# Moving the slices of a dense projection one step later among the attention steps that they fill

## Chip, cores and metric

The kernel runs on one core of one Trainium2 chip. The metric is the device time of one execution in microseconds (us), as the median of several runs.

## What is computed

One inference step of a two-layer encoder trunk, for two groups of requests (512 prompt frames and 32 sample frames) that share one set of weights. In each layer the mixer sub-layer makes one wide input projection and feeds it to three branches; cross-attention and a dense feed-forward follow. The part that matters here is the first branch, attention with a forget gate, over 8 heads of 64, and the input projection beside it:

```python
a_q, a_k, a_v, a_f, b_q, b_k, b_v, c_in, gate_in = _split_cols(h @ w_in, IN_SPLITS)
...
log_f = jax.nn.log_sigmoid((a_f + fox_forget_bias).astype(f32))
d_all = jnp.cumsum(jnp.concatenate([fox_lf0.astype(f32), log_f], axis=1), axis=1)
...
s = jnp.einsum('bqhd,bkhd->bhqk', qb, k_all).astype(jnp.float32) * scale
s = s + jnp.swapaxes(dqb, 1, 2)[:, :, :, None] - d_k[:, :, None, :]
mask = kpos[None, None, None, :] <= pb[:, None, :, None]
p = jax.nn.softmax(jnp.where(mask, s, -jnp.inf), axis=-1)
return jnp.einsum('bhqk,bkhd->bqhd', p.astype(v_all.dtype), v_all)
```

Only the columns `a_q, a_k, a_v, a_f` of the input projection are needed by this branch. The columns of the other two branches are computed later, and the kernel calls them the late projection.

## The kernel before

The program is written by hand for each engine: each engine has its own list of instructions, in order, and the lists meet only at semaphores. Nothing reorders the work, so the place of a call in the Python loops is its place in its engine's queue.

**The attention stage.** Heads go in pairs, four pairs (`it` = 0 to 3) in each of two layers. A pair has ten score tiles, `FOX_TILES`: for each of its two heads four blocks of 128 prompt queries (against 128, 256, 384, 512 keys) and one of 32 sample queries (against 544 keys). TensorE (PE) goes through 13 steps, k = 0 to 12:

- `fox_prologue(k)` in steps 0 and 1: three groups of transposes ("jobs": L882, L887, L891) that bring a head's values, keys and cached keys into place. ScalarE (ACT) copies each group out of PSUM. Jobs alternate between banks 4 and 5, so each waits for the copy of the job two before it (`fx_put`).
- `fox_scores(k)` in steps 0 to 9 (L904, L905, L910 to L912). The first tile of a head waits for `fx_scaled`, the scaling of that head's queries by VectorE (DVE), L2136.
- `late(s)`: a slice of the late projection, below.
- `fox_turn(k - 2)` in steps 2 to 11: transposes of the normalised probabilities (L922, L926).
- `fox_values(...)` in steps 4, 7, 8, 10 and 12 (L940, L945, L948): the products with the values. Each waits for ACT's copies of the turned probabilities.

Between PE's steps DVE takes each tile's maximum (`fox_max`, L2122), ACT the exponentials (`fox_exp`, L1423), and DVE the division by the sum (`fox_norm`, L2129, L2131). After a pair, DVE copies its output to `brT` (`fox_evac`, L2141, L2142).

**The late projection.** It has 26 units of 128 output columns. Of each, every half of the frames is one accumulation in bank 7 of PSUM, in two slices of 12 matmuls (L858). ACT copies a finished half out (`late_put(q)`, L1426), and the next half may not begin before that (`late_evac`). Each unit's weights are split by DVE into a high and a low part (`late_split`, L1932 and L1942) into one of two buffers, so a unit's split waits for the last slice of the unit two before it (`late_done`). Twelve slices go with each pair. Slice 0 of pair 0 is ahead of the loop.

**In the first pair only**, DVE also clears rows of the second set of buffers at step 3, behind the split that stands there (L2158, L2159).

**DVE's order at a pair's end** is: the last split of the pair (`late_split(3 * it + 2)`), `fox_evac`, then `fox_scale(0)` of the next pair, which `fox_scores(0)` of that pair waits for.

Of the kernel before, what the change touches and what calls it, by code (L numbers as in the profile page):

```python
# [162 lines left out]
def build_program(nc, A, C_const, C_rope, O):  # L163
# [7 lines left out]
    with ExitStack() as ctx:  # L171
# [257 lines left out]
        def half(t, h):  # L429
            return t[:, h * HT:(h + 1) * HT]  # L430
# [221 lines left out]
        def _(pe):  # L652
# [142 lines left out]
            for l in range(DEPTH):  # L795
# [6 lines left out]
                def of_h_split(k):  # L802
                    return HH[:, k, :], hTR[:, k, :]
# [42 lines left out]
                def late(s):  # L846

                    n, h, k0 = s // 4, s % 4 // 2, s % 2 * 4
                    v = V_LATE + n
                    if k0 == 0:  # L850
                        if h == 0:
                            pe.wait_ge(split_done, l * SPLITS + v + 2)
                        pe.wait_ge(late_evac, l * 2 * N_LATE + 2 * n + h + 1)
                    for k in range(k0, k0 + 4):
                        xhi, xlo = of_h_split(k)
                        whi, wlo = (w[:, v % 2, k, :] for w in (WHI, WLO))
                        for i, (w, x) in enumerate(((whi, xhi), (whi, xlo), (wlo, xhi))):
                            ins = mm(PS[:, 7, 0:HT], w, half(x, h), start=(k == 0 and i == 0), stop=(k == 7 and i == 2))  # L858
                    if k0 == 4:
                        ins.then_inc(late_done, 1)  # L860
# [5 lines left out]
                for it in range(FOX_HEADS // 2):  # L866
# [49 lines left out]
                    def fox_turn(k):  # L916
                        h, i = FOX_TILES[k]
                        pe.wait_ge(fx_norm, g * 10 + k + 1)
                        b = put_bank()
                        if i < 4:  # L920
                            for t in range(i + 1):
                                ins = tr(b[:, t * P:(t + 1) * P], FP[:, k % 3, t * P:(t + 1) * P], ident)  # L922
                        else:
                            for t in range(5):
                                w = P if t < 4 else DEC_SEQ
                                ins = tr(b[0:w, t * 32:(t + 1) * 32], FP[0:32, k % 3, t * P:t * P + w],  # L926
                                         ident[0:32, 0:32])
                        ins.then_inc(fx_turned, 1)
# [24 lines left out]
                    for k in range(13):  # L953
                        if k < 2:
                            fox_prologue(k)
                        if k < 10:
                            fox_scores(k)
                        if k < (12 if it else 11):
                            late(12 * it + k + (0 if it else 1))
                        if 2 <= k <= 11:  # L960
                            fox_turn(k - 2)
                        if k in FOX_VALUES:
                            fox_values(FOX_VALUES[k])
# [457 lines left out]
        def _(act):  # L1421
# [3 lines left out]
            def copy(out, in_):  # L1425
                return act.copy(out, in_)  # L1426
# [62 lines left out]
            for l in range(DEPTH):  # L1489
# [45 lines left out]
                def late_put(q):  # L1535

                    act.wait_ge(late_free, l * 2 * N_LATE + q + 1)
                    act.wait_ge(late_done, l * 2 * N_LATE + q + 1)
                    copy(ESTL[:, q % 4, :], PS[:, 7, 0:HT]).then_inc(late_evac, 1)

                for it in range(FOX_HEADS // 2):
                    g = l * 4 + it
                    job = [0]

                    def next_job():
                        j = job[0]
                        job[0] += 1
                        act.wait_ge(fx_turned, g * 16 + j + 1)
                        return PS[:, 4 + j % 2, :]

                    def fox_prologue(h):
                        for to in (FVT, FKT):
                            b = next_job()
                            copy(to[it % 2][:, h, 0:4, :].rearrange("p a b -> p (a b)"), b[:, 0:256])
                            copy(to[it % 2][0:DEC_SEQ, h, 4, :], b[0:DEC_SEQ, 256:320])
                            act.drain().then_inc(fx_put, 1)
                        b = next_job()
                        copy(FK[it % 2][0:64, h, T:T + PAST], b[0:64, :]).then_inc(fx_put, 1)

                    def fox_exp(k):  # L1560
                        i = FOX_TILES[k][1]
                        act.wait_ge(fx_max, g * 10 + k + 1)
                        m, n = (P, (i + 1) * P) if i < 4 else (DEC_SEQ, T)
                        f(FP[0:m, k % 3, 0:n], bank_on(k % 3)[0:m, 0:n], ACT.Exp, bias=FST[0:m, k % 3, 0:1],
                          accum_out=FST[0:m, k % 3, 1:2])
                        act.drain().then_inc(fx_exp, 1)

                    def fox_put(k):
                        i = FOX_TILES[k][1]
                        b = next_job()  # L1570
                        if i < 4:
                            copy(FPT[:, FOX_SLOT[k], 0:(i + 1) * P], b[:, 0:(i + 1) * P]).then_inc(fx_put, 1)
                        else:
                            copy(FPT[:, FOX_SLOT[k], 0:P], b[:, 0:P])
                            copy(FPT[0:32, FOX_SLOT[k], P:P + 32], b[0:32, P:P + 32])
                            act.drain().then_inc(fx_put, 1)

                    for k in range(12):
                        if k < 2:
                            fox_prologue(k)  # L1580
                        if k < 10:
                            fox_exp(k)
                        if k % 2 == (1 if it else 0):
                            late_put(6 * it + k // 2)
                        if k >= 2:
                            fox_put(k - 2)

# [284 lines left out]
        def _(dve):  # L1873
# [148 lines left out]
            for l in range(DEPTH):  # L2022
# [92 lines left out]
                for it in range(FOX_HEADS // 2):  # L2115
                    g = l * 4 + it

                    def fox_max(k):
                        h, i = FOX_TILES[k]
                        m, n = (P, (i + 1) * P) if i < 4 else (DEC_SEQ, T)  # L2120
                        dve.wait_ge(fx_scores, g * 10 + k + 1)
                        dve.tensor_reduce(FST[0:m, k % 3, 0:1], bank_on(k % 3)[0:m, 0:n], AX.X, ALU.max,  # L2122
                                          negate=True).then_inc(fx_max, 1)

                    def fox_norm(k):
                        h, i = FOX_TILES[k]
                        m, n = (P, (i + 1) * P) if i < 4 else (DEC_SEQ, T)
                        dve.wait_ge(fx_exp, g * 10 + k + 1)
                        dve.reciprocal(FST[0:m, k % 3, 2:3], FST[0:m, k % 3, 1:2])  # L2129
                        dve.drain()  # L2130
                        ts(FP[0:m, k % 3, 0:n], FP[0:m, k % 3, 0:n], FST[0:m, k % 3, 2:3], None, ALU.mult) \  # L2131
                            .then_inc(fx_norm, 1)

                    def fox_scale(h):
                        dve.wait_ge(fx_loaded[it % 2][h], (l * 2 + it // 2 + 1) * 16 * 7)
                        ts(FQ[it % 2][0:64, h, :], FQ[it % 2][0:64, h, :], HEAD_DIM ** -0.5, None, ALU.mult).then_inc(fx_scaled, 1)  # L2136

                    def fox_evac():

                        dve.wait_ge(fx_out, g + 1)  # L2140
                        copy(brT[:, it, 0:SEQ], PS[:, 6, :])  # L2141
                        copy(brT[:, it, SEQ:T], PS[:, 3, 64:96])  # L2142
                        dve.drain().then_inc(fx_evac, 2)

                    for k in range(11):
                        if k < 2:
                            fox_scale(k)
                        if k < 10:
                            fox_max(k)
                        if k >= 1:  # L2150
                            fox_norm(k - 1)
                        if k in (3, 9):
                            late_split(3 * it + k // 9)
                        if (it, k) == (0, 3):

                            dve.wait_ge(est_free, l * 12 + 16)
                            dve.wait_ge(lf_stored, (l + 1) * 64)
                            dve.memset(FQ[1][64:66, :, :], 1.0)  # L2158
                            dve.memset(FK[1][64:66, :, :], 1.0)  # L2159
                            dve.drain().then_inc(fx_rows, 1)  # L2160
                    late_split(3 * it + 2)
                    fox_evac()
# [703 lines left out]
```

## Time and profile before

| | |
|---|---|
| median of 3 runs | 2830.41 us (2828.62 to 2831.1) |
| the profiled execution's own time | 2827.76 us |
| its span, first to last instruction | 2826.0 us |
| mean granted TensorE clock | 0.992 |
| PE busy | 2703.9 us, 96% of the span |
| DVE busy | 1686.9 us, 60% |
| ACT busy | 756.6 us, 27% |
| POOL (GpSimd) busy | 244.8 us, 9% |

A row of the profile names an engine, a line of the kernel, the operation, what it writes and reads, and how many instructions were merged into it. In brackets stands how long the engine sat idle before it, and who released it.
### The profile page before, as it was taken

The page shows a single profiled execution, that of the slowest core. Times are in us where ns is not written, and L with a number is a line of the kernel's source. Part 1 is how long each engine was busy: PE and PEld are TensorE (multiplying, and loading weights), DVE is VectorE, ACT ScalarE, POOL GpSimd, SP SyncE. Part 2 cuts the span into 40 slices and gives each one's busy share as a digit, 9 for nine tenths or more (in the row PEclk, how much of TensorE's full clock was granted, in tenths as well). Part 3 has the DMA queues.
Part 4 walks back from the last instruction along what each step waited for, and adds up shares of the span by engine and source line. Part 5 has one row for each costly group of instructions (what it writes and reads, how often), then busy time and mean ns, then how long its engine had stood idle before and what let it go on. Part 6 is the DMA issues. An engine that isn't in the chain of part 4 may idle for free.

```text
span 2826.0 us, 63638 instructions
## 1 busy us (share of the span) xinstructions
PE 2703.9 (96%) x26656; PEld 2539.9 (90%) x26656; DVE 1686.9 (60%) x3101; ACT 756.6 (27%) x1813; POOL 244.8 (9%) x423
## 2 busy tenths in 40 slices
PE   8999999999999989999999999999999998999998
PEld 7877889999999789999988788899999996999998
DVE  6544565666666476664484455556666656666634
ACT  2143343333232330000123433433233324200001
POOL 1221112000000100000002221110000000000000
PEclk9999999999999999999999999999999999999999
DMA  5543436222263222333335444442224532233331
GB/s 159 143 126 105 141 107 168 73 73 66 83 172 112 56 82 86 87 88 89 83 98 139 111 136 138 84 157 73 73 69 117 155 98 75 71 87 90 87 89 59
DMA packets 421293, 290.29 MB, mean 103 GB/s; under 512 B 38560, under 2 KB 387392, under 8 KB 420880
## 3 DMA queue, kind: packets, MB, share of 16 engines
q1 hardware_dynamic: 399024, 228.64, 29.3%
q0 software_dynamic: 21984, 57.59, 6.5%
q8 instruction: 211, 3.46, 0.5%
q14 instruction: 74, 0.61, 0.1%
HBM read 232.12 MB, written 54.07 MB: 101 GB/s over the span
## 4 chain that ended last, share of the span: by engine, by line
PE 76%; DVE 11%; DVEq 4%; ACT 3%; DMA 3%; issue 2%; ACTq 0%; SPq 0%
PE PS L762 35%; PE PS L858 10%; PE PS L1161 8%; PE PS L1094 7%; DMA U<-gate_scratch 2%; ACT U L1423 2%; PE PS L904 1%; PE PS L1135 1%; PE PS L1303 1%; PE PS L783 1%; ACT U L1426 1%; DVE WLO L1942 1%; PE PS L940 1%; DVE U_r L1932 1%; PE PS L1019 1%
## 5 line engine op out<-in xcount | busy, mean ns | idle before, releaser
L762 PE MATMUL PS<-U_r,WHI 128*128 128x272 f32 x3008 | 538.5, 290 | 17.0 <-DVEq L2449 9.5
L1932 DVE CAST WHI<-ring 128x1024 fp32r<-128x1024 f32 (+2 forms) x262 | 175.3, 669 | 485.2 <-PE PS L762 372.2
L762 PEld LDWEIGHTS PS<-U_r,WHI 128*128 128x128 f32 x3008 | 438.5, 189 | 23.8 <-DVEq L2449 13.8
L1426 ACT COPY U<-PS 128x272 f32<-128x272 f32 (+8 forms) x770 | 267.5, 372 | 661.8 <-PE PS L1161 140.0
L762 PE MATMUL PS<-brT_r,WHI 128*128 128x272 f32 x1920 | 398.1, 289 | 7.5 <-DVEq L1944 6.1
L762 PE MATMUL PS<-U_r,WLO 128*128 128x272 f32 x1728 | 357.1, 288 | 0.0
L762 PE MATMUL PS<-hT_r,WHI 128*128 128x272 f32 x1600 | 330.6, 288 | 0.0
L1942 DVE TENSOR_TENSOR WLO<-ring,WHI 128x1024 fp32r<-128x1024 f32 (+2 forms) x262 | 308.3, 1177 | 20.6 <-issue 0.9
L762 PE MATMUL PS<-brT_r,WLO 128*128 128x272 f32 x1536 | 318.3, 289 | 0.0
L762 PEld LDWEIGHTS PS<-brT_r,WHI 128*128 128x128 f32 x1920 | 301.5, 188 | 10.1 <-DVEq L1944 7.6
L858 PE MATMUL PS<-U_r,WHI 128*128 128x272 f32 x832 | 260.7, 313 | 12.3 <-ACT U L1426 12.1
L762 PEld LDWEIGHTS PS<-U_r,WLO 128*128 128x128 f32 x1728 | 271.5, 189 | 0.0
L762 PEld LDWEIGHTS PS<-hT_r,WHI 128*128 128x128 f32 x1600 | 251.6, 189 | 0.0
L858 PE MATMUL PS<-U_r,WLO 128*128 128x272 f32 x832 | 241.1, 290 | 0.0
L858 PE MATMUL PS<-hT_r,WHI 128*128 128x272 f32 x832 | 240.2, 289 | 0.0
L762 PEld LDWEIGHTS PS<-brT_r,WLO 128*128 128x128 f32 x1536 | 239.9, 189 | 0.0
L1094 PE MATMUL PS<-U_r,WHI 128*128 128x272 f32 x768 | 230.1, 300 | 2.8 <-DVEq L2244 2.4
L1094 PE MATMUL PS<-U_r,WLO 128*128 128x272 f32 x768 | 221.6, 289 | 0.0
L1094 PE MATMUL PS<-hT_r,WHI 128*128 128x272 f32 x768 | 220.9, 288 | 0.0
L1161 PE MATMUL PS<-U 64*64 64x64 f32 (+1 forms) x5184 | 213.2, 239 | 0.0
L1161 PEld LDWEIGHTS PS<-U 64*64 64x64 f32 x5184 | 207.2, 134 | 1.2 <-issue 0.6
L858 PEld LDWEIGHTS PS<-U_r,WHI 128*128 128x128 f32 x832 | 158.5, 190 | 31.4 <-issue 15.0
(351 smaller groups left out, 4106.0 us busy)
## 6 DMA issues: line engine op xcount, KB each, us to landing
ring<-in_w_in_dram SPq DMA_DIRECT2D x126, 512.0 KB, 4.4
ring<-in_w_ffn_in_dram SPq DMA_DIRECT2D x88, 512.0 KB, 3.8
ring<-in_w_ffn_out_dram SPq DMA_DIRECT2D x32, 448.0 KB, 3.5
proj_scratch<-U POOLq DMA_DIRECT2D x104, 136.0 KB, 2.1
U<-proj_scratch SPq DMA_DIRECT2D x48, 272.0 KB, 4.7
ring<-in_w_branch_dram SPq DMA_DIRECT2D x48, 256.0 KB, 3.3
gate_scratch<-U POOLq DMA_DIRECT2D x88, 136.0 KB, 3.2
U<-gate_scratch SPq DMA_DIRECT2D x44, 272.0 KB, 2.9
```

Of the source, the lines that this page charges most:

```text
L762: ins = mm(PS[:, 2 * q + h, 0:HT], w, half(x, h), start=(first and k == 0 and n == 0), stop=(last and k == kn - 1 and n == len(terms) - 1))
L783: ins = mm(PS[:, 2 * j + h, 0:HT], w, half(x, h), start=(k == 0 and n == 0), stop=(k == KM - 1 and n == 2))
L858: ins = mm(PS[:, 7, 0:HT], w, half(x, h), start=(k == 0 and i == 0), stop=(k == 7 and i == 2))
L904: mm(PS[:, b, 0:n], q, FK[it % 2][0:66, h, 0:n], start=True, stop=False)
L940: ins = mm(PS[o, 6, i * P:(i + 1) * P], FVT[it % 2][:, h, t, :], pt[:, t * P:(t + 1) * P], start=(t == 0), stop=(t == i))
L1019: mm(PS[:, b, 0:n], DQ[h][r, i * P:(i + 1) * P], DK[h][r, 0:n], start=True, stop=False)
L1094: ins = mm(PS[:, 6 + h, 0:HT], w, half(x, h), start=(k == 0 and i == 0), stop=(k == 7 and i == 2))
L1161: ins = mm(PS[r, bank, cols], w_c[r], x_c[r], start=(n == 0), stop=(n == len(pairs) - 1))
L1423: return act.activation(out, in_, func, **kw)
L1426: return act.copy(out, in_)
L1932: copy(hi, src)
L1942: tt(lo, w, hi.bitcast(F32), ALU.subtract)
```

## The change

The slices of a pair are moved among PE's steps. In pairs 1 to 3 they stood in steps 0 to 11 and now stand in steps 1 to 12. In pair 0 they stood in steps 0 to 10 and now stand in steps 2 to 12. Their number and order are the same. A slice now stands in front of the values of step 12. ACT's copies of the finished halves follow: they were in the odd steps (even ones in pair 0) and are now in steps 2, 4, ... 12 of each pair. The pair's first split on DVE goes from step 3 to step 5; the other two keep their places.

```diff
@@ PE @@
-                        if k < (12 if it else 11):
-                            late(12 * it + k + (0 if it else 1))
+                        if k >= (1 if it else 2):
+                            late(12 * it + k - 1)
                         if 2 <= k <= 11:
                             fox_turn(k - 2)
                         if k in FOX_VALUES:
@@ ACT @@
-                    for k in range(12):
+                    for k in range(13):
                         if k < 2:
                             fox_prologue(k)
                         if k < 10:
                             fox_exp(k)
-                        if k % 2 == (1 if it else 0):
-                            late_put(6 * it + k // 2)
-                        if k >= 2:
+                        if k >= 2 and k % 2 == 0:
+                            late_put(6 * it + k // 2 - 1)
+                        if 2 <= k < 12:
                             fox_put(k - 2)
@@ DVE @@
-                        if k in (3, 9):
+                        if k in (5, 9):
                             late_split(3 * it + k // 9)
```

## Rows read from the trace of the kernel before

**Rows 1.** The page: the chain that ended last, by engine.

```profile
PE 76%; DVE 11%; DVEq 4%; ACT 3%; DMA 3%; issue 2%; ACTq 0%; SPq 0%
```

**Rows 2.** Windows, the attention stage of each layer: busy us, then clock, DMA share, GB/s.

```profile
107.21:263.81 156.60, 147.16 (x1187) 120.98 (x1185) 73.79 (x163) 62.68 (x193) 34.91 (x57) 0.99 0.44 120
1503.53:1660.41 156.88, 147.09 (x1186) 120.98 (x1184) 73.73 (x163) 62.77 (x193) 34.92 (x57) 0.99 0.43 120
```

**Rows 3.** Waits of PE in layer 0's stage: us in total, times, longest.

```profile
PE PS L858 <- ACT U L1426: 3.3, 4, 2.5
PE PS L940 <- ACT U L1426: 2.7, 4, 0.7
```

**Rows 4.** Timeline of PE, end of pair 1 and start of pair 2.

```profile
181.07 0.39 PE L858 MATMUL PS<-U_r,WHI 128*128 128x272 f32 x1 [0.25 <-ACT U L1426]
...
185.63 0.60 PE L922 MATMUL PS<-CB,U 128*128 128x128 f32 x4
186.90 1.09 PE L940 MATMUL PS<-U 128*64 128x128 f32 x16 [0.68 <-ACT U L1426]
187.93 0.52 PE L882 MATMUL PS<-CB,U 64*128 64x64 f32 x5
...
189.49 0.44 PE L904 MATMUL PS<-U 66*128 66x128 f32 x2
...
189.80 0.37 PE L858 MATMUL PS<-U_r,WHI 128*128 128x272 f32 x1
...
191.47 0.52 PE L882 MATMUL PS<-CB,U 64*128 64x64 f32 x5
...
192.57 0.63 PE L891 MATMUL PS<-CB,U 128*64 128x128 f32 x4 [0.27 <-ACTq L1556]
```

**Rows 5.** Timeline of DVE over the same stretch.

```profile
185.83 0.69 DVE L1932 CAST WHI<-ring 128x1024 fp32r<-128x1024 f32 x1 [2.77 <-PE PS L858]
186.60 1.23 DVE L1942 TENSOR_TENSOR WLO<-ring,WHI 128x1024 fp32r<-128x1024 f32 x1
188.04 0.69 DVE L2141 COPY brT<-PS 128x512 f32<-128x512 f32 x1 [0.22 <-PE PS L940]
...
188.95 0.43 DVE L2136 TENSOR_SCALAR U<-U 64x544 f32<-64x544 f32 x1
```

**Rows 6.** Timeline of ACT over the same stretch.

```profile
190.62 0.19 ACT L1423 ACTIVATION_READ_ACCUMULATOR U<-PS,U 128x1 f32 x1
192.03 1.03 ACT L1426 COPY U<-PS 128x256 f32<-128x256 f32 x4 [1.22 <-PE PS L882]
```

**Rows 7.** Timelines of DVE and then PE, pair 0 of layer 0, from step 3.

```profile
121.53 0.68 DVE L1932 CAST WHI<-ring 128x1024 fp32r<-128x1024 f32 x1
...
123.94 0.96 DVE L2158 MEMSET U<- 2x1088 f32 x1 [0.44 <-issue]
125.30 1.82 DVE L2159 MEMSET U<- 2x2112 f32 x1 [0.39 <-issue]
...
128.84 0.39 PE L858 MATMUL PS<-U_r,WHI 128*128 128x272 f32 x1 [2.50 <-ACT U L1426]
```

**Rows 8.** Timeline of DVE, pair 1, steps 5 and 6.

```profile
167.26 0.35 DVE L2131 TENSOR_SCALAR U<-U 128x256 f32<-128x256 f32 x1
169.04 0.56 DVE L2122 TENSOR_REDUCE U<-PS 128x1 f32<-128x384 f32 x1 [1.42 <-PE PS L905]
```

**Rows 9.** Windows of layer 0 and 1: PE, PEld, DVE, ACT, POOL busy, then the granted clock.

```profile
126.79:130.20 3.41, 1.36 (x11) 1.36 (x12) 2.22 (x7) 1.98 (x7) 0.56 (x1) 1.00 0.38 102
130.20:133.61 3.41, 3.41 (x14) 2.62 (x13) 0.91 (x3) 0.76 (x2) 0.00 (x0) 0.51 0.76 197
358.89:362.30 3.41, 2.87 (x24) 2.02 (x22) 2.14 (x3) 0.65 (x4) 0.00 (x0) 1.00 0.03 5
362.30:365.71 3.41, 3.41 (x17) 3.07 (x18) 2.38 (x7) 1.66 (x6) 0.00 (x0) 0.51 0.86 225
1505.76:1512.58 6.82, 5.30 (x51) 4.81 (x52) 2.09 (x7) 3.91 (x14) 2.98 (x5) 1.00 0.20 61
```

## Prediction, made before the changed kernel was timed

> **What bounds the kernel now.** I read the page first. The chain that ended last is 76% PE, with DVE at 11% [rows 1], so time is won or lost where PE waits. I then cut out the two stretches in which the attention stage runs: they take 156.60 and 156.88 us, and PE is busy for 147.16 and 147.09 of them [rows 2]. The two layers agree to 0.3 us, so what one pair shows in layer 0 may be counted twice. Only about 9.5 us of each stage are not PE work. No change of order can win more than this, apart from what the clock gives back, and the moved slices take as long as before. The list of waits tells what fills the gap [rows 3]: the values wait four times for ACT, 2.7 us in all, and slices wait four times for ACT's copy of bank 7, 3.3 us in all, of which one wait is 2.5. Last I read the timelines around a pair's end, because there the change takes cover away on one side and adds it on the other.
>
> **The change, part by part** (each pair is one of 4, each layer one of 2).
>
> *The wait in front of the last values.* The last turn begins at 185.63 and the values of step 12 at 186.90, after 0.68 us of idleness [rows 4]. PE waits for ACT's copy of what it has just turned. A slice takes 1.67 us (189.80 to 191.47 [rows 4]), so it hides that wait wholly. Eight pairs: -5.4 us.
>
> *The wait in step 10.* In pairs 1 to 3 the slice at 181.07 waits 0.25 us for the copy of bank 7 [rows 4]; with the 2.5 of pair 0 these three make up the 3.3 [rows 3]. In step 10 ACT's copy sat behind the exponential of tile 9. Now the half ends in step 10, where no exponential is left, so the copy is early. Six times: -1.5 us.
>
> *Pair 0, step 3.* DVE does the split from 121.53, then clears two blocks, the second until 127.12, and only then goes on to tile 4's maximum. PE's slice waits 2.50 us until 128.84 [rows 7]. The slice in this step keeps its parity, so it still needs the same copy, but the split now stands in step 5. From its rows [rows 5] a split takes 2.00 us (185.83 to 187.83). So the wait falls to about 0.5 us: 2 x -2.0 = -4.0 us. Behind this wait the clock was at the lower level: 0.51 in 130.20:133.61, with PE busy throughout [rows 9]. Half of 3.41 us is 1.7; I take 1.6 a time, a little less, since idle moments within it lose nothing: -3.2 us for two.
>
> *The first scores of the next pair.* This is the cost. The last split of a pair waits for the pair's last slice, and that slice now ends right in front of the last values. Let T be the moment at which PE leaves it. In the trace before that moment is 185.63, the split begins 0.20 later and ends at T + 2.2 [rows 4, 5]. Behind it on DVE are `fox_evac` and then `fox_scale(0)`. With 0.1 for the drain (the cast and the subtraction stand 0.08 apart), evacuation begins at T + 2.3. The scaling begins 0.91 after that (188.04 to 188.95) and takes 0.43 [rows 5]: the queries are ready at T + 3.65, and PE can go on at T + 3.7. PE itself needs 1.03 for the values (186.90 to 187.93) and 1.56 for the prologue (187.93 to 189.49) [rows 4]: it is there at T + 2.6. Before, the split ran under the last turn and the wait; now it is late, by 1.1 us. Pairs 1 to 3 in both layers: 6 x 1.1 = +6.6 us. The last pair pays nothing: the stage behind it begins with a slice and matmuls that need no scaled queries.
>
> *The second prologue.* Behind the first scores (189.49 to 189.80) there was a slice, which hid DVE's maximum and ACT's exponential. ACT is strictly in order, and the second prologue's third job needs ACT's copy of its first. ACT is done with the exponential at 190.81 [rows 6], 1.32 after the scores began. With 0.1 for the drain and 0.54 for the copy (192.03 to 192.57 [rows 4, 6]), the job begins 1.95 after them. Without that wait it would begin at 0.31 + 1.10 = 1.41. So 0.55 us is lost, in pair 0 too: 8 x 0.55 = +4.4 us. ACT's next copies and tile 1's exponential are queued behind it, and PE has a slice or the long scores of step 2 in front of what needs them: nothing more.
>
> *The split in step 5.* DVE was idle for 1.42 us in front of tile 6's maximum [rows 8]. It ends its previous work at 167.61; the split takes 2.0, so this maximum comes 0.6 us late, and with it the exponential, the copy of bank 7 behind it and the slice of step 7 that needs it. The cost lies between 0 (the slack in front of that slice) and 0.6; I take 0.2, as the copy waited for is some 0.4 ahead now. In pair 0 everything on DVE is already late before this. Six times: +1.2 us, between 0 and 3.6.
>
> *Queues passed.* No DMA is moved in SP's list. POOL's stores of finished halves wait for ACT's copies and follow them by a step. The last of a pair still comes before POOL's wait for the evacuation, so the buffers' release isn't later than that. The weights' loads wait for the splits; the moved split feeds a unit needed only in step 9. I count nothing for them. Were that cover gone, a load would be late by one step, 2 to 3 us, once.
>
> Sum: -5.4 - 1.5 - 4.0 - 3.2 + 6.6 + 4.4 + 1.2 = **-1.9 us**.
>
> *The clock at the new pair starts.* From T to the next slice PE would have 1.03 + 1.56 + 1.1 + 0.3 + 1.1 + 0.55 + 0.8, some 6.4 us of small matmuls with 2.2 us of waits in them. Before there was a slice in the middle. The rows are of two minds [rows 9]. After 126.79:130.20, with PE busy for 1.36, the clock fell to 0.51; and after 358.89:362.30 it did so too, though PE was busy for 2.87, with small work. In 1505.76:1512.58, the start of pair 0 of layer 1, PE stood still for 1.5 of 6.82 and the clock stayed at 1.00. A new start has a worse stretch than that in it and a better one than the first. I take two falls out of six starts, at 1.6 each: +3.2 us. The ends are none and six (+9.6).
>
> The Trainium skill, TensorE: Matmul & The Clock Gate, section "A second HAM failure mode: psum-queue depth-cycling", speaks against this change: frequent small idle gaps of PE between groups of matmuls can make the clock swing between its levels. The trace agrees in part, with the fall to 0.51 behind 358.89:362.30, and disagrees at 1505.76. By that rule every start would pay; the second rival below is that case.
>
> Together -1.9 + 3.2 = **+1.3 us**, from 2827.76 to 2829.1 for the profiled execution. That one stood 2.65 us below the median, so the median is **2831.7, given as 2832 us**.
>
> **The rivals.**
> 1. *No fall of the clock.* The sum stays at -1.9: 2828.5 us. It isn't apart from my forecast in kind. Both are no change: a measurement of this kernel can tell about 0.2%, 5.7 us.
> 2. *The clock decides, slower.* The place is the stretch from T to the second scores of pairs 1 to 3. With five or more falls, each 1.6 (or two long ones in a start), the sum is -1.9 + 8.0 or more: 2836.5 to 2838 us. It decides from five falls on. For it: more than 2 us of waits in each start. Against: the stretch is broken by matmuls everywhere, and 0.95 us of waits at each start before cost no fall.
> 3. *The first scores don't wait.* If DVE were earlier than I say, the +6.6 is gone, and with no falls the sum is -8.5: 2822 us, faster. Against: the split needs the last slice, in the code, and DVE's queue is in order.
> 4. *The wait in front of the last values stays* (the change doesn't do what it says): ACT's copy would have to be more than a slice late. Then +5.4: 2837 us. The copy needs 1.3 from the turn's start, and a slice with the turn covers 2.2.
>
> **How the numbers follow.** My forecast with rival 1, no more than four falls: 0.74. Rival 2: 0.12; rival 4 and other losses, such as a longer wait in step 7 (+3.6 at most): 0.04. Rival 3: 0.04; falls avoided elsewhere and a pair 0 that wins its whole wait (-1 more): 0.06. So faster 0.10, same 0.74, slower 0.16. The range reaches from 2825 (the sum with -3.5 for the last case) to 2838 (six falls).
>
> **What would show it.** In the profile after: no idle time in front of the last L940 of a pair; the first L904 of pairs 1 to 3 waits about 1.1 us for DVE's L2136; L891 of the second prologue waits about 0.8 in place of 0.27; the 2.50 wait of pair 0 is near 0.5 and the clock behind it at 1.00; the stage takes 156.6 - 1 us plus 1.6 per fall. I am wrong if the first scores wait far from 1.1 us, if the clock falls at nearly every start, or if the stage after this one gives back or takes what this one won.

## The result, and the profile after

The changed kernel took 2846.27 us in the median of 5 runs (2840.11 to 2855.29), against 2831.1 for the kernel before. The ratio is 1.0048, with a 95% interval from 1.0028 to 1.0069: slower, by some 13.6 us (the two medians are 15.2 us apart). A second measurement of the same kernel gave 1.0064 (1.0045 to 1.0083). The forecast was 2832 us, no change, with 2838 as its upper end.

The page of the changed kernel first: its span, busy times and the chain by engine. The profiled execution took 2843.98 us.

```profile
span 2842.2 us, 63638 instructions
...
PE 2723.9 (96%) x26656; PEld 2554.2 (90%) x26656; DVE 1687.4 (59%) x3101; ACT 757.5 (27%) x1813; POOL 244.9 (9%) x423
...
PE 76%; DVE 12%; DVEq 4%; ACT 3%; DMA 3%; issue 2%; ACTq 0%; SPq 0%
```

The span is 16.2 us longer and PE is busy for 20.0 us more (2723.9 against 2703.9), on the same number of matmuls, 26656. A wait would add to the span and not to the busy time; here the matmuls themselves have become slower. So the clock is what to look at. These are windows of the changed kernel over the attention stage of each layer, now taken from the first prologue to the start of the last `fox_evac`. The columns are those of [rows 2].

```profile
109.56:268.27 158.71, 151.06 (x1181) 124.02 (x1182) 71.81 (x161) 62.40 (x192) 34.80 (x57) 0.96 0.43 119
1510.28:1674.03 163.75, 157.94 (x1181) 128.76 (x1182) 71.76 (x160) 62.44 (x192) 35.11 (x57) 0.91 0.43 115
```

The same stretches took 153.87 and 153.88 us before, at 0.99. So the stages are 4.8 and 9.9 us longer, 14.7 of the 16.2, at a mean clock of 0.96 and 0.91. The two layers were alike before and are not now, though they run the same program: the waits differ little between them, and the clock much.

The moments at which DVE starts to copy a pair's output show it pair by pair. First two rows of the kernel before, from layer 1:

```profile
1584.74 0.69 DVE L2141 COPY brT<-PS 128x512 f32<-128x512 f32 x1 [0.22 <-PE PS L940]
1622.67 0.69 DVE L2141 COPY brT<-PS 128x512 f32<-128x512 f32 x1 [0.22 <-PE PS L940]
```

and the same rows of the changed kernel:

```profile
1550.98 0.69 DVE L2141 COPY brT<-PS 128x512 f32<-128x512 f32 x1
1592.03 0.69 DVE L2141 COPY brT<-PS 128x512 f32<-128x512 f32 x1
1633.06 0.69 DVE L2141 COPY brT<-PS 128x512 f32<-128x512 f32 x1
1674.03 0.69 DVE L2141 COPY brT<-PS 128x512 f32<-128x512 f32 x1
```

A pair took 37.93 us before. Here it takes 41.05, 41.03 and 40.97. In layer 0 the three later pairs took 40.02, 38.50 and 40.03.

What lies in these pairs is in the windows of low clock, with the columns of [rows 9]:

```profile
150.25:153.66 3.41, 1.84 (x18) 1.51 (x19) 1.32 (x5) 1.97 (x7) 2.37 (x4) 1.00 0.43 124
153.66:157.07 3.41, 3.41 (x17) 3.10 (x17) 0.65 (x3) 1.04 (x3) 0.21 (x1) 0.50 0.92 234
1512.10:1522.30 10.20, 10.00 (x44) 7.42 (x43) 2.95 (x11) 4.49 (x15) 3.14 (x5) 0.50 0.17 46
1552.96:1559.78 6.82, 6.44 (x31) 5.06 (x32) 1.28 (x5) 2.43 (x9) 2.17 (x4) 0.51 0.81 214
1594.00:1600.80 6.80, 6.47 (x31) 5.11 (x32) 1.28 (x5) 2.43 (x9) 2.19 (x4) 0.51 0.87 207
1635.00:1641.70 6.70, 6.43 (x32) 5.07 (x32) 1.28 (x5) 2.47 (x9) 2.21 (x4) 0.51 0.97 302
```

Behind the first row, in which PE was busy for 1.84 of 3.41 us, the clock goes to its lower level. It does so at five of the six starts of later pairs; only the start near 191 stays up. Both pair-0 starts fall too, that of layer 0 for some 6.8 us (112.8 to 119.6) and that of layer 1 for 10 us. The low stretches of the later pairs differ in length: about 3.4 us in layer 0, some 6.8 in layer 1.

The waits are where the forecast had them. The list of PE's waits in layer 0, as in [rows 3]:

```profile
PE PS L891 <- ACTq L1556: 3.8, 8, 0.7
PE PS L904 <- DVE U L2136: 2.6, 3, 0.9
PE PS L858 <- ACT U L1426: 1.3, 4, 0.6
```

The row of the last values (L940) is gone. The timeline of PE at the start of pair 2, to be held against [rows 4]:

```profile
187.52 1.09 PE L940 MATMUL PS<-U 128*64 128x128 f32 x16
...
189.63 0.63 PE L891 MATMUL PS<-CB,U 128*64 128x128 f32 x4 [0.28 <-ACTq L1556]
191.13 0.49 PE L904 MATMUL PS<-U 66*128 66x128 f32 x2 [0.87 <-DVE U L2136]
...
193.14 0.63 PE L891 MATMUL PS<-CB,U 128*64 128x128 f32 x4 [0.71 <-ACTq L1556]
```

and that of DVE, against [rows 5]:

```profile
187.62 0.69 DVE L1932 CAST WHI<-ring 128x1024 fp32r<-128x1024 f32 x1 [4.21 <-PE PS L858]
188.39 1.23 DVE L1942 TENSOR_TENSOR WLO<-ring,WHI 128x1024 fp32r<-128x1024 f32 x1
189.74 0.69 DVE L2141 COPY brT<-PS 128x512 f32<-128x512 f32 x1
...
190.64 0.44 DVE L2136 TENSOR_SCALAR U<-U 64x544 f32<-64x544 f32 x1
```

The last values no longer wait. The first scores wait 0.87 us for the scaling, which stands behind the late split. And the third job of the second prologue waits 0.71. By the Trainium skill, TensorE: Matmul & The Clock Gate, section "Architectural detail: the array is 16× 32×32, not 1× 128×128", ACT and DVE take their queues strictly in order; the four rows of DVE stand one behind the other, though the scaling needs nothing from the split: in the experiment that puts it in front, the wait is gone.

### The profile page after: what moved, and what is told of

The parts are those of the page before. It is cut to its first block, busy times and chain, and to the rows that moved or that the text cites. A ratio compares the mean times of both kernels' runs of the same rounds, so it can differ in the third digit from the quotient of the medians.

```text
span 2842.2 us, 63638 instructions
## 1 busy us (share of the span) xinstructions
PE 2723.9 (96%) x26656; PEld 2554.2 (90%) x26656; DVE 1687.4 (59%) x3101; ACT 757.5 (27%) x1813; POOL 244.9 (9%) x423
## 4 chain that ended last, share of the span: by engine, by line
PE 76%; DVE 12%; DVEq 4%; ACT 3%; DMA 3%; issue 2%; ACTq 0%; SPq 0%
PE PS L762 35%; PE PS L858 10%; PE PS L1161 8%; PE PS L1094 7%; DMA U<-gate_scratch 2%; ACT U L1423 2%; DVE WLO L1942 1%; PE PS L1135 1%; PE PS L1303 1%; PE PS L783 1%; PE PS L904 1%; DVEq L1941 1%; ACT U L1426 1%; PE PS L1019 1%; DVE U_r L1932 1%
```

## The experiments

Times are ratios to the kernel before on the same chip. "Stages" is the sum of both layers' attention stages in the profiled execution, measured as above; it is 307.75 us for the kernel before. In kernels where a pair's last slice is late, the last copy starts some 1 us later for the same work of PE, and the stage behind gives this back. Falls of the clock are counted in the one profiled execution of each kernel.

**The change in the first pair alone.** Pairs 1 to 3 are as before.

```diff
-                        if k >= (1 if it else 2):
-                            late(12 * it + k - 1)
+                        if (k >= (1 if it else 2)) if it == 0 else (k < (12 if it else 11)):
+                            late(12 * it + (k - 1 if it == 0 else k + (0 if it else 1)))
...
-                        if k >= 2 and k % 2 == 0:
-                            late_put(6 * it + k // 2 - 1)
+                        if (k >= 2 and k % 2 == 0) if it == 0 else (k < 12 and k % 2 == (1 if it else 0)):
+                            late_put(6 * it + (k // 2 - 1 if it == 0 else k // 2))
...
-                        if k in (5, 9):
+                        if k in (3 if it else 5, 9):
```

> The change in pair 0 of each layer alone; pairs 1 to 3 as before. Both pair-0 starts of the changed kernel showed the lower clock, so the clock theory expects the gain of the shorter wait in step 3 (2 x 2.0), of the clock behind it (3.2) and of the wait before the last values (1.4), less 1.1 for the second prologue, to be eaten by two falls at the starts worth 3.4 to 5 each: between -1 and +3 us against the kernel before. The rival, that only the waits themselves count, expects -7 to -8 us, 2823.

Measured: 0.9994 (0.9982 to 1.0006), no change. The windows over its stages, layer 0 then 1:

```profile
110.45:261.48 151.03, 144.26 (x1173) 118.50 (x1174) 71.42 (x160) 62.27 (x192) 34.38 (x57) 1.00 0.45 125
1507.74:1661.65 153.91, 147.14 (x1173) 120.36 (x1174) 71.43 (x161) 62.37 (x192) 34.39 (x57) 0.98 0.44 123
```

In layer 0 the clock stayed up and the stage won 2.84 us. In layer 1 it fell from 1510 to 1517 and the win was gone. In one execution the two layers show both cases.

**The change in the later pairs alone.** Pair 0 is as before.

```diff
-                        if k >= (1 if it else 2):
-                            late(12 * it + k - 1)
+                        if (k >= (1 if it else 2)) if it > 0 else (k < (12 if it else 11)):
+                            late(12 * it + (k - 1 if it > 0 else k + (0 if it else 1)))
...
-                        if k >= 2 and k % 2 == 0:
-                            late_put(6 * it + k // 2 - 1)
+                        if (k >= 2 and k % 2 == 0) if it > 0 else (k < 12 and k % 2 == (1 if it else 0)):
+                            late_put(6 * it + (k // 2 - 1 if it > 0 else k // 2))
...
-                        if k in (5, 9):
+                        if k in (5 if it else 3, 9):
```

> The change in pairs 1 to 3 of each layer alone; pair 0 as before. The waits by themselves add up to +4.5 us against the kernel before: -4.1 (values), -1.5 (step 10), +5.2 (first scores, 0.87 x 6 as measured), +2.6 (third job, 0.43 x 6), +1.2 to +2 (the split in step 5). The clock theory adds falls at most of the six starts, 1.7 to 3.4 each, and expects +10 to +18 us, 2841 to 2849. The rival without the clock stays at +4 to +5, 2835.

Measured: 1.0021 (1.0008 to 1.0034), +6 us, between the two expectations. In the profiled execution four of six starts fell. Its stages add up to 320.64 us, +12.9, and its later pairs without a fall took 38.54 us as those of the changed kernel did. The ratio alone would not have told waits from clock; the next runs do.

**The first split alone.** The kernel before, with only pair 0's split moved.

```diff
-                        if k in (3, 9):
+                        if k in (3 if it else 5, 9):
```

> The kernel before with nothing changed but the place of pair 0's first split on VectorE, from step 3 to step 5. It tells what this part is worth with no new start. If the 2.50 us wait becomes 0.5 and the clock stays up behind it: -7 us, 2824. If the wait only moves to a later slice: within 1 us of before.

Measured: 0.9973 (0.996 to 0.9986), -7.6 us: the part that the forecast put at -7.2. Stages 301.98 us, although the start of pair 0 in layer 1 fell in its profiled execution.

**Useless matmuls at the later pairs' starts.** TensorE is given work where it waits.

```diff
+                    def filler(n):
+                        for _ in range(n):
+                            mm(PS[:, 7, 384:512], identb[:, :], mfoxb[:, :], start=True, stop=True)
...
+                        if k == 0 and it > 0:
+                            filler(14)
                         if k < 10:
                             fox_scores(k)
+                        if k == 0 and it > 0:
+                            filler(12)
```

> The changed kernel with 26 useless 128-column bf16 matmuls added at the start of each of pairs 1 to 3: 14 in front of the first scores, where TensorE waits 0.87 us, and 12 behind them, where it waits for ScalarE; their results go to unused columns of bank 7 and are never read. The clock theory expects the clock to stay up at these six starts and the time to fall by some 8 to 13 us against the changed kernel although TensorE has more to do: 2833 to 2838. The rival, that the waits and not the clock cost the time, expects no gain, or 1 to 3 us more than the changed kernel: 2847 to 2849.

Measured: 1.0014 (1.0005 to 1.0024), against 1.0048 and 1.0064 for the changed kernel: about 10 us faster with 156 matmuls more. PE's timeline at the start of pair 1 of layer 1, where line 955 is the filler:

```profile
1558.52 0.95 PE L955 MATMUL PS<-mfoxb,identb 128*128 128x128 bf16 x14
1559.55 0.49 PE L904 MATMUL PS<-U 66*128 66x128 f32 x2
1559.94 0.83 PE L955 MATMUL PS<-mfoxb,identb 128*128 128x128 bf16 x12
```

The first block fills the 0.87 us in front of the scores. None of the six starts fell. Each later pair took 38.73 to 38.77 us, 0.25 more than one of the changed kernel without a fall (38.50), and 2.3 less than one with a long fall. Both pair-0 starts, which had no filler, still fell.

**The same in every pair.** Pair 0 gets 14 such matmuls in front of its first prologue and 12 on either side of its first scores.

```diff
+                            mm(PS[:, 7 if it else 6, 384:512], identb[:, :], mfoxb[:, :], start=True, stop=True)
...
+                    if it == 0:
+                        filler(14)
...
+                        if k == 0:
+                            filler(14 if it else 12)
                         if k < 10:
                             fox_scores(k)
+                        if k == 0:
+                            filler(12)
```

> The changed kernel with the useless matmuls at the start of every pair, pair 0 too: there 14 in front of the first prologue, where TensorE waits about 1.2 us for VectorE, and 12 on either side of the first scores (into bank 6; bank 7 holds half a result). In the first such kernel both pair-0 starts still fell to the lower clock. If the falls are all that is left of the loss, they go too, and with them another 3 to 5 us each: 0.998 to 0.9995 against the kernel before, which is where the waits alone would put the change with pair 0's gain. If the pair-0 starts fall in spite of it, the time stays near 1.0014.

Measured: 0.9996 (0.9987 to 1.0006). The whole loss is gone.

```profile
110.45:264.88 154.43, 150.73 (x1285) 125.52 (x1284) 71.54 (x159) 62.33 (x192) 34.35 (x57) 1.00 0.44 122
1506.24:1660.64 154.40, 150.70 (x1285) 125.51 (x1284) 71.77 (x159) 62.37 (x192) 34.38 (x57) 1.00 0.44 122
```

Both stages are at 1.00 and alike again. With 102 useless matmuls in each, they are 4.3 and 9.4 us shorter than those of the changed kernel. Each layer has 14 more in front of its stage. They begin when PE's wait there has ended (1.26 us in layer 0, 1.61 in layer 1), so they don't fill it, and they cost some 0.9 us a layer on top. Part of the profile's gain lies elsewhere: the stage behind in layer 1, where no filler stands, is 4.35 us shorter than in the changed kernel, for a reason given at the end of the next section.

**The changed kernel again.** The same kernel beside the second group of experiments.

> The changed kernel itself, beside the others of this group and against the kernel before: 1.003 to 1.007 again, as in its first measurement.

Measured: 1.0064 (1.0045 to 1.0083), with stages of 324.83 us in its profiled execution, 17.1 over those of before. Five of six starts of later pairs fell again. Layer 0 shows both kinds: pairs 1 and 2 took 39.93 and 40.00 us, and pair 3, whose start kept the clock, 38.51. The three of layer 1 took 40.99, 40.97 and 40.97.

**Scaling before the split.** The changed kernel without the 0.87 us wait.

```diff
-                    late_split(3 * it + 2)
+                    if it == 3:
+                        late_split(3 * it + 2)
                     fox_evac()
...
                             fox_norm(k - 1)
+                        if k == 1 and it > 0:
+                            late_split(3 * it - 1)
```

> The changed kernel, but VectorE does a pair's last split only in step 1 of the next pair, behind the output's copy and the scaling of the first queries (the last pair keeps its order). This takes away the 0.87 us wait of the first scores, six times, and nothing else. Waits alone: -5 us against the changed kernel. With the clock theory, the stretch without a slice gets shorter and denser, so some falls go too: -6 to -12 us against the changed kernel, still above the kernel before, since the start has no slice and the third job still waits. If it equals the kernel before or better, the missing slice was not the cause but the wait alone.

Measured: 0.9995 (0.9985 to 1.0006). Its start still has no slice, and the third job still waits 0.62. Yet only one of its six later starts fell, and the other later pairs but the last of each layer took 37.46 and 37.76 us, less than before. Both pair-0 starts, which this edit does not touch, fell for 10 us. I had put it above the kernel before; it equals it. So in the later pairs a missing slice alone seldom brings a fall, as far as one execution tells: it took the missing slice and the wait together.

**Slices at both ends.** The starts keep their slices; only the last slice goes in front of the last values.

```diff
-                        if k >= (1 if it else 2):
-                            late(12 * it + k - 1)
+                        if k < (11 if it else 10):
+                            late(12 * it + k + (0 if it else 1))
+                        if k == 12:
+                            late(12 * it + 11)
...
-                        if k in (5, 9):
+                        if k in (3 if it else 5, 9):
```

ACT's copies stay as in the kernel before but for the last, which goes to step 12. The first split is in step 5 in pair 0, as in "the first split alone", and in step 3 in the others.

> Slices in steps 0 to 10 (0 to 9 in pair 0) as before and only the last one of each pair in step 12, in front of the last values; pair 0's first split in step 5. The last split of a pair is then as late as in the changed kernel, so the first scores wait 0.87 us six times (+5.2), but a slice follows them. Gains: values 8 x 0.68, and the split of pair 0, which measured 0.9973 alone (-7.7). The theory that a fall needs a start without a slice expects no falls at the six starts and -8 us against the kernel before, 0.997. The rival, that the wait in front of the scores alone brings the fall, expects six falls or so, and 0 to +4.

Measured: 0.9995 (0.9985 to 1.0004); I expected 0.997. One of its six later starts fell, so the wait without the missing slice is no regular cause either. But the gain did not come, and the first split alone (0.9973) was some 6 us quicker. This kernel's later pairs without a fall took 38.24 us, 0.31 longer than before: the late split costs the first scores more than the last values win. Stages 307.80.

**Both ends, split deferred.** The same, with the last split done in step 1 of the next pair.

```diff
-                    late_split(3 * it + 2)
+                    if it == 3:
+                        late_split(3 * it + 2)
                     fox_evac()
...
                             fox_scale(k)
+                        if k == 1 and it > 0:
+                            late_split(3 * it - 1)
                         if k < 10:
                             fox_max(k)
```

> As the one before it, and VectorE does a pair's last split in step 1 of the next pair, behind the first tile's maximum, under the slice of step 0 (the last pair keeps its order). If the 0.87 us wait goes and nothing takes its place: -13 us against the kernel before, 0.9955, and the quickest of all. If the split is now in the way of tile 1's maximum, it gives back up to 1 us a pair: 0.9975.

Measured: 0.997 (0.9959 to 0.998), 2822.66 us: faster than both kernels, and of a size with the first split alone (0.9973), whose interval overlaps.

```profile
109.63:258.97 149.34, 144.90 (x1181) 119.52 (x1182) 71.47 (x161) 62.25 (x192) 34.96 (x57) 1.00 0.46 126
1503.38:1654.05 150.67, 146.39 (x1181) 120.90 (x1182) 71.23 (x160) 62.36 (x192) 34.98 (x57) 0.99 0.45 125
```

These are the shortest stages of all, 300.01 us, and pair 1 takes 37.15. None of its later pairs' starts fell; that of pair 0 in layer 1 did. The part between this profile's -7.7 in the stages and the -13 that I expected is not explained in full: that fall is one piece of it, and a wait of 0.8 us of the turns (L922) for DVE's division in pair 0 of each layer, which the kernel above has too, is another. So no order of the slices that was tried is clearly quicker than the first split's move by itself.

**The split back in step 3.**

```diff
-                        if k in (5, 9):
+                        if k in (3, 9):
```

> The changed kernel with only the first split of each pair moved back from step 5 to step 3. It would then wait in step 3 for a slice that TensorE does in step 4, and tile 4's maximum, its exponential and ScalarE's copy of bank 7 would come behind it: about 2 us of waiting in front of the slice of step 5 in each of eight pairs, and the clearing of rows on top in pair 0, so 15 to 30 us more than the changed kernel. If the split's new place is what cost the time, the kernel gets faster instead.

Measured: 1.0169 (1.0154 to 1.0185), some 35 us over the changed kernel's median of the first measurement and 30 over that of the second. The split's new place is not what cost the time. All eight of its starts fell too, so part of the 30 to 35 us is the clock. In the old place the split waits for a slice of step 4, and the slice of step 5 for all behind it:

```profile
176.91 0.57 PE L858 MATMUL PS<-U_r,WHI 128*128 128x272 f32 x1 [1.94 <-ACT U L1426]
```

## Why the prediction was wrong, by its steps

*The last values and step 10* were right: neither wait is left in the list.

*Pair 0, step 3* was right in this execution: the wait is 0.59 us (0.5 forecast) and the clock is at 1.00 there. In the second profiled execution of the changed kernel the wait in layer 0 was 0.72 us, and the clock fell behind it once more. The row of the changed kernel, against the last of [rows 7]:

```profile
126.66 0.36 PE L858 MATMUL PS<-U_r,WHI 128*128 128x272 f32 x1 [0.59 <-ACT U L1426]
```

*The first scores* wait 0.87 us, not 1.1. I had let the split begin 0.20 after PE left the slice and it begins 0.10 after; and PE is through with the prologue 2.74 us after it began the last values (187.52 to 190.26), where I had 2.6. *The second prologue* waits 0.44 us more than before (0.71 less the 0.27 of [rows 4]), where I had 0.55. *The split in step 5* costs 0.23 in pair 1, against 0.2. Together these put a later pair at -0.68 - 0.25 + 0.87 + 0.44 + 0.23 = +0.61 us. Measured, where the clock stays up: 38.50 - 37.93 = +0.57. That is 3.4 us for six pairs, where the forecast had 5.5: in the waits it was right, and a little too dark.

*The step that failed is "The clock at the new pair starts"*: "I take two falls out of six starts, at 1.6 each". There were five out of six in each of two executions, and four of six in the kernel with only the later pairs changed: 14 of 18. (The kernel with the split back in step 3, whose starts are the same, adds six of six.) The price was right for a short fall, 40.02 - 38.50 = 1.5 us, and too small for the long ones of layer 1, 2.5 us (41.02 - 38.50). So the six starts cost 2 x 1.5 + 3 x 2.5 = 10.6 us in the profiled execution (with unrounded prices), not 3.2. And I did not count the starts of pair 0 at all, though the change takes the slices of two steps from there: their falls stood in the sum as nothing. Over all kernels in which that start has no slice and no filler in steps 0 and 1, it fell 9 times in 10, not counting the kernel with the split back in step 3. With its slices it fell 4 times in 10, all four in layer 1, and each for no more than some 3.5 us, against 6.8 to 10.4 without. Pair 0 won its 2.0 us and the clock behind it, and lost them at its start: 40.16 and 40.70 us after, 40.04 and 40.08 before. The one such pair whose start kept the clock, in layer 0 of the kernel with the first pair alone, took 37.19 us. So these two falls cost 3.0 and 3.5 us, some 6.5 together. In the profiled execution the clock at the eight starts thus cost about 17 us where the forecast had 3.2, and this gap of some 14 us is nearly the whole miss.

My second rival named the mechanism and its place, and said that it decides from five falls on. Its time, 2836.5 to 2838 us, was too low for the same two reasons: long falls cost more than 1.6, and pair 0 was left out. What else was wrong was its chance, 0.12, and the reason given against it, that 0.95 us of waits at each start before had cost no fall. Those waits had a slice behind them. Of the Trainium skill's rule that I weighed there, the section "A second HAM failure mode: psum-queue depth-cycling" of TensorE: Matmul & The Clock Gate, the trace now agrees for the most part: no single wait within the later pairs' starts is longer than 0.87 us, and the clock went down and up again at five of these six. One start kept it, so not every start pays. The pair-0 starts, both of which fell, are a weaker case, since PE also stands still for 1.20 and 1.56 us right in front of them.

That the falls make the loss is shown by the useless matmuls: more work for PE, stages at 1.00, and 0.9996. The stage behind adds something of its own. In layer 0 it was 0.6 us shorter and in layer 1 3.2 us longer, with a fall (1751 to 1758) behind the wait for `cache_diff_v`. These are that wait in layer 1 of the kernel before, of the changed kernel, and of the kernel with fillers in every pair:

```profile
1739.15 1.19 PE L982 MATMUL PS<-U,CB 128*128 128x272 f32 x4 [2.50 <-DMA U<-in_cache_diff_v_dram]
1751.75 2.18 PE L982 MATMUL PS<-U,CB 128*128 128x272 f32 x4 [2.75 <-DMA U<-in_cache_diff_v_dram]
1737.02 1.19 PE L992 MATMUL PS<-U,CB 128*128 128x272 f32 x4 [1.42 <-DMA U<-in_cache_diff_v_dram]
```

The clock stayed up behind the first and the third. The second profiled execution of the changed kernel has the fall too, behind a wait of 2.71 us. But the wait alone does not decide it: in the kernel with both ends and the split deferred it was 3.34 us and the clock stayed up. Whether the change brought that fall or only its moment did was not tried.

Pair 0's start at its old slices falls in some executions and not in others. That this is what spreads the kernel before from 2828.69 to 2841.39 over 31 runs was not tried.

## What to carry to other kernels

A piece of work that fills one wait can also be what keeps TensorE's clock up where it stands. Before it is moved, add up the waits that are left in the stretch it leaves: two waits under 1 us each, with only small matmuls between, cost 1.5 to 2.5 us a time here, more than the wait that the move took away. And a slice that another engine's next step waits for should not be the last one in front of a boundary, unless that step is put behind what the next stretch needs first.

If busy time grows on the same instructions, look at the granted clock before the waits. Useless matmuls in the waits are a quick test: if the kernel gets faster with them, the clock is the cause.

## What was not expected of the hardware

The fall repeats at the same place of each pair in layer 1, with pairs of 41.05, 41.03 and 40.97 us, in both profiled executions of the changed kernel (40.99, 40.97 and 40.97 in the second). In layer 0 falls came at two of three such starts. The program is the same, so what stands in a start does not by itself decide whether it falls; that its moment does was not tried. Among the later pairs' starts, those with a slice and the 0.87 us wait of the first scores fell once in six, and those with neither slice nor this wait once in six. Those without a slice and with the wait fell 14 times in 18. Each of the first two counts comes from one profiled execution.
